# A mixture-of-experts block: one visit loop split in two, with the routed bias products made at the split

## The chip, the core and the metric

The kernel runs on one core of a Trainium2 chip. The core's engines run side by side, each with its own queue: TensorE (PE) multiplies into eight PSUM banks, VectorE (DVE) and ScalarE (ACT) work on vectors, GpSimd (POOL) issues gathers and scatters, SyncE (SP) issues the large transfers. They meet through semaphores. The metric is the device time of one execution in microseconds (us); lower is better. A difference of under 0.3% (4.2 us) can't be told from none here.

## What is computed

One hybrid decoder layer on 512 tokens of 1024 values. Its first part (a gated DeltaNet group and a convolution group) ends before the stretch that matters here. The second part is a mixture of 32 experts, of which each token uses four:

```python
logits = (xt @ w_router + b_router)
top_val, top_idx = lax.top_k(logits, TOP_K)
gates = jax.nn.softmax(top_val, axis=-1)
...
hid = x_blk @ w_gate_up[e] + b_gate_up[e]        # 1024 x 2048 weights per expert
gate, up = hid[:, :D_FF], hid[:, D_FF:]
...
return ((up + 1.0) * glu) @ w_down[e] + b_down[e]  # 1024 x 1024 weights per expert
...
y = jax.ops.segment_sum(weighted, row_tok, num_segments=t + 1)[:t]  # sum of gate * expert output
```

All data are float32. Every expert's 12.6 MB of weights is read once, 402 MB in all. The bias of the down projection, weighted by the gates, doesn't depend on the experts' products: summed over a token's experts it is `gates (512 x 32) @ b_down (32 x 1024)`. These are the **routed bias products**.

## The kernel before

The experts are handled in **visits**. Visit i multiplies expert i's gate/up weights (`gate_up(i)`, line 2138, matmuls in line 2136) and then expert i-1's down weights (`down(i - 1)`, line 2200, matmuls in line 2189). A visit's tokens lie in up to four groups of 32; groups 2 and 3 are skipped where the expert has too few tokens, so visits differ in length on PE. Visit 0 stands alone, visits 1 to m = 30 are one hardware loop on each engine, and the last expert, 31, is handled behind it.

- **SP** issues the weights in a fixed order: for a visit four gate/up pieces c0, c2, c4, c6 of 2 MB into `ring`, then two down pieces of 2 MB (chunk pairs u 0-1 and 2-3) into `dslots`. Each issue waits until PE has used what stood in that slot one expert ago (semaphores `gu_used`, `d_used`), so at most one expert's weights are under way or unused at a time. Behind the loop the order is c0, c2 of expert 31 (these are its first two waits), the down pieces of expert 30, c4, c6, then expert 31's down weights as four pieces of 1 MB. Then come four "planes": 2 MB each of the scattered expert outputs, read back for the final sum (lines 463, 465, 468, and 471 as four tiles).
- **PE** runs `gate_up`, waits for `act_ready`, runs `down`. Bank 6 also takes the small products that turn the routing into row numbers (`idx_mm`, line 2100, between c4 and c6 of a visit), which DVE reads right after (lines 1510 to 1514).
- **DVE** makes row numbers, transposes the gate/up results (line 1575) and the next tokens (1488), and computes the activation; its last step of a visit (line 1615) waits for the down products of the expert before.
- **ACT** makes the sigmoid (line 1007) and scales the down results out of banks 4 and 5 (line 1001, `results`).
- **POOL** gathers tokens and scatters results (lines 621, 626).

The routed bias products need `gates_turn` (four transposes of the gates, line 2111, into bank 7), a copy by ACT (line 1018), and for each of the four token tiles two matmuls into banks 6 and 7 (`routed_bias`, line 2122) and two additions by DVE into `x2` (`add_bias`, lines 1552 and 1553). Since both banks are used again for each tile, PE waits for the additions of the tile before (`acc_ready`). In the kernel before all of it stands behind the loop, among the last expert's gate/up products, while SP's last weights are still arriving.

Of the kernel before, what the change touches and what calls it, by code (L numbers as in the profile page):

```python
# [33 lines left out]
GROUPS = 4  # L34
CAP = GROUP * GROUPS
STAGES = 4


def block_kernel(nc, x, attn_norm_w, w_in, gdn_conv_w, gdn_a_log, gdn_dt_bias, gdn_norm_w, cf_dw_w, cf_dw_b,
# [10 lines left out]
    T = SEQ // P  # L50
# [21 lines left out]
    with ExitStack() as ctx:  # L72
# [98 lines left out]
        def take(*dims):  # L171
# [117 lines left out]
        gt_done, gt_copied, bd_done, acc_ready = (sem(n) for n in ("gt_done", "gt_copied", "bd_done", "acc_ready"))  # L289
        hot_ready, idx_done, idx_ready, gathered, xt_ready = (sem(n) for n in (  # L290
            "hot_ready", "idx_done", "idx_ready", "gathered", "xt_ready"))
# [60 lines left out]
        def tokens_left(engine, i):  # L352

            return engine.value_load(left[0:1, bass.ds(i, 1)], min_val=0, max_val=SEQ)
# [364 lines left out]
        def _(act):  # L719
# [275 lines left out]
            m = visits_less_two(act)  # L995

            def results(stage):

                gates = slot_gate.rearrange("p s g -> p (s g)")
                for g in range(GROUPS):  # L1000
                    ins = A(yb[:, g, :], bank[4 + g // 2][:, (g % 2) * QD:(g % 2 + 1) * QD], ACT.Copy,  # L1001
                            scale=gates[:, bass.ds(stage * GROUPS + g, 1)])
                ins.then_inc(y_ready, 1)
# [5 lines left out]

            act.sem_inc(y_ready, 1)  # L1010
            sigmoid_gate(1)
            with act.Fori(1, m + 1) as i:
                sigmoid_gate(i + 1)
                act.wait_ge(d_used, i * 4 + 4)
                act.wait_ge(landed, i * 16)
                results((i - 1) % STAGES)
            act.wait_ge(gt_done, 1)
            A(GT, bank[7][0:E, :], ACT.Copy).then_inc(gt_copied, 1)
            act.wait_ge(d_used, m * 4 + 8)
            act.wait_ge(landed, m * 16 + 16)  # L1020
            results((E - 2) % STAGES)
# [23 lines left out]
        def _(dve):  # L1045
# [504 lines left out]
            def add_bias(t):  # L1550
                dve.wait_ge(bd_done, t + 1)
                V.tensor_tensor(x2[:, t, 0:HALF], BIAS_PAIR[0][:, :], x2[:, t, 0:HALF], ALU.add)
                V.tensor_tensor(x2[:, t, HALF:D], BIAS_PAIR[1][:, :], x2[:, t, HALF:D], ALU.add
                                ).then_inc(acc_ready, 1)
# [11 lines left out]
            m = visits_less_two(dve)  # L1566
# [19 lines left out]
            def act_part(e, visit, base):  # L1586

                s = own.s
                c = base
                dve.wait_ge(hid_ready, visit * GROUPS + GROUPS)  # L1590

                def biased(out, half):
                    bias = bgu[:, half * KC:(half + 1) * KC, bass.ds(e, 1)]
                    bias = bias.rearrange("p b o -> p (b o)").rearrange("p (b o) -> p b o", o=1)
                    for g in range(GROUPS):
                        V.tensor_tensor(out[:, g, :].rearrange("p (b s) -> p b s", b=KC),  # L1596
                                        hidT[:, g, half, :].rearrange("p (b s) -> p b s", b=KC),
                                        bias.to_broadcast([P, KC, GROUP]), ALU.add).then_inc(s, 1)

                biased(g2, 0)  # L1600
                c = c + GROUPS
                dve.wait_ge(s, c)
                V.tensor_scalar(g2, g2, LIMIT, None, ALU.min).then_inc(g2_ready, 1)  # L1603
                biased(u2, 1)
                c = c + GROUPS
                dve.wait_ge(s, c)
                V.tensor_scalar(u2, u2, LIMIT, -LIMIT, ALU.min, ALU.max).then_inc(s, 1)
                c = c + 1
                dve.wait_ge(sg_ready, visit)
                V.tensor_tensor(g2, g2, sg, ALU.mult).then_inc(s, 1)  # L1610
                c = c + 1
                dve.wait_ge(s, c)
                dve.wait_ge(d_used, visit * 4)
                flat = lambda v: v.rearrange("p g n -> p (g n)")
                V.scalar_tensor_tensor(out=flat(actT), in0=flat(u2), scalar=1.0, in1=flat(g2), op0=ALU.add,  # L1615
                                       op1=ALU.mult).then_inc(act_ready, 1)
# [2 lines left out]
            LOOP_OWN = STEPS_IDX + STEPS_ACT  # L1619
            act_part(0, 1, own.n)  # L1620
            own.n += STEPS_ACT
            with dve.Fori(1, m + 1) as i:
                base = (i - 1) * LOOP_OWN + own.n
                dve.wait_ge(idx_done, i + 3)
                dve.wait_ge(rows_known, i * 2 + 1)
                numbers(base, (i + 2) % STAGES)

                e3 = (i + 3) % E
                hot(e3)
                dve.wait_ge(hot_ready, (i + 4) * (T + 1) - 1)  # L1630
                lower(e3)
                hid_turn(i + 1)
                xt_turn(i + 1)
                act_part(i % E, i + 1, base + STEPS_IDX)

            def last_act():

# [44 lines left out]
                        turn_at[g + 1] = turn(g + 1)  # L1682
                    product(g)

            for t in range(T):
                add_bias(t)
            dve.wait_ge(gu_used, m * KC + 2 * KC)
            dve.wait_ge(d_used, m * 4 + 4)
            last_act()
# [28 lines left out]
        def _(pe):  # L1718
# [389 lines left out]
            def gates_turn():  # L2108
                pe.wait_ge(cnt_read, 1)
                for t in range(T):  # L2110
                    ins = TR(bank[7][0:E, t * P:(t + 1) * P], Gm[:, t, :], ident)
                ins.then_inc(gt_done, 1)
# [83 lines left out]
            def down(i, tokens):  # L2196
                for u in range(4):
                    if u == 1:
                        pe.wait_ge(slot_in[8 + u], 16)
                    elif u % 2 == 0:  # L2200
                        pe.wait_ge(slot_in[8 + u], i * 16 + 16)
                    with pe.If(tokens > 2 * GROUP):
                        down_mm(u, 2)
                        with pe.If(tokens > 3 * GROUP):
                            down_mm(u, 3)
                    down_mm(u, 0)
                    down_mm(u, 1).then_inc(d_used, 1)
# [1 line left out]
            tokens = tokens_left(pe, 0)  # L2209
            pe.wait_ge(xt_ready, 1)  # L2210
            gate_up(0, first=True, known=tokens)
            with pe.Fori(1, m + 1) as i:
                pe.wait_ge(xt_ready, i + 2)
                gate_up(i)
                pe.wait_ge(act_ready, i)
                pe.wait_ge(y_ready, i)
                tokens = tokens_left(pe, i - 1)
                down(i - 1, tokens)
            tokens = tokens_left(pe, m + 1)
            pe.wait_ge(xt_ready, m + 3)  # L2220
            pe.wait_ge(idx_ready, m + 3)
            gates_turn()
            gate_up(m + 1, pairs=(0,), known=tokens)
            routed_bias(0)
            gate_up(m + 1, pairs=(2,), known=tokens)
            routed_bias(1)
            pe.wait_ge(act_ready, m + 1)
            pe.wait_ge(y_ready, m + 1)
            down(m, tokens_left(pe, m))
            routed_bias(2)  # L2230
            gate_up(m + 1, pairs=(4,), known=tokens)
            routed_bias(3)
            gate_up(m + 1, pairs=(6,), known=tokens)

            def last_down(u, g):
                w = view(ring, u * SLOT, 2, D)
# [57 lines left out]
```

## Time and profile before

| | |
|---|---|
| median of three runs | 1394.98 us (1392.49 to 1396.18) |
| span of the profiled execution | 1395.8 us |
| PE busy | 1241.0 us (89%), of it line 2136 566.6, line 2189 284.7 |
| DVE, POOL, ACT busy | 679.5, 320.3, 223.3 us |
| moved by DMA | 455.33 MB, 326 GB/s over the span |
| PE idle until gate/up weights, down weights | 56.2, 21.8 us |
| granted TensorE clock, mean | 0.973 of 2.4 GHz |

The profile is of one execution, and its span runs from the first to the last instruction; the page gives no other time for it. It lies 0.8 us above the median and within the range of the runs. Its times within the span are used as they are, and differences found in them are applied to the median. In the rows, a timeline row has its start and its length in us, then engine, line, operation, tiles and count, and in square brackets how long the engine had been idle and what released it. PE's matmul ends are modelled.

### The profile page before, as it was taken

How to read it: one execution, taken by the hardware profiler on the slowest of the kernel's cores; microseconds unless marked ns; L12 is line 12 of the kernel's file. 1: busy time of each engine (PE TensorE's matmuls, PEld its weight loads, DVE VectorE, ACT ScalarE, POOL GpSimd, SP SyncE). 2: the span in 40 equal slices, each digit the busy share in tenths (PEclk: the TensorE clock that was granted, in tenths of full speed). 3: DMA queues.
4: the chain of work that ended last, by engine and by line, in shares of the span. 5: the costliest groups of instructions: out<-in, count | busy, mean ns of one | idle time of the engine just before them, and what ended most of it. 6: DMA issues, size and time to landing. Idle time of an engine off the chain costs nothing.

```text
span 1395.8 us, 32044 instructions
## 1 busy us (share of the span) xinstructions
PE 1241.0 (89%) x12814; PEld 585.9 (42%) x12815; DVE 679.5 (49%) x1360; ACT 223.3 (16%) x439; POOL 320.3 (23%) x432
## 2 busy tenths in 40 slices
PE   6999999999599999899899999798978887879992
PEld 3444454564235554353534445233432332335331
DVE  2898885444644364335434433345443334353428
ACT  3125543412100011000000100000110000001103
POOL 5001111000322224222223212222233222222221
PEclk9999999999799999999999999999999999999996
DMA  9212000312589999999999999999999999999996
GB/s 307 85 61 91 1 31 1 142 74 86 210 337 400 409 418 424 425 426 426 426 425 425 424 426 425 426 426 425 426 424 425 426 427 425 426 426 426 380 407 245
DMA packets 59374, 455.33 MB, mean 326 GB/s; under 512 B 13308, under 2 KB 23604, under 8 KB 34214
## 3 DMA queue, kind: packets, MB, share of 16 engines
q1 hardware_dynamic: 44262, 432.59, 74.8%
q0 software_dynamic: 11568, 18.92, 3.7%
q10 hardware_dynamic: 3504, 3.26, 0.9%
q8 instruction: 28, 0.46, 0.1%
q14 instruction: 12, 0.10, 0.0%
HBM read 445.02 MB, written 14.81 MB: 329 GB/s over the span
## 4 chain that ended last, share of the span: by engine, by line
PE 58%; DMA 29%; DVE 7%; issue 2%; ACT 2%; ACTq 1%; POOL 0%; SPq 0%; DVEq 0%; POOLq 0%
PE bank L2136 26%; DMA ring<-in_w_gate_up_dram 15%; PE bank L2189 14%; DMA dslots<-in_w_down_dram 14%; PE bank L1797 6%; PE bank L1987 4%; DVE dslots L1122 3%; PE bank L1792 2%; DVE hbuf L1697 1%; PE bank L1865 1%; PE bank L1872 1%; PE bank L2100 1%; PE bank L2122 1%; PE bank L1952 1%; PE bank L1956 1%
## 5 line engine op out<-in xcount | busy, mean ns | idle before, releaser
L2136 PE MATMUL bank<-ring,wq 128*32 128x512 f32 x4992 | 566.6, 601 | 64.9 <-DMA ring<-in_w_gate_up_dram 56.2
L2136 PEld LDWEIGHTS bank<-ring,wq 128*32 128x32 f32 x4992 | 208.8, 111 | 381.1 <-issue 344.3
L2189 PE MATMUL bank<-dslots,intra 128*32 128x256 f32 x5056 | 284.7, 380 | 22.6 <-DMA dslots<-in_w_down_dram 21.8
L2189 PEld LDWEIGHTS bank<-dslots,intra 128*32 128x32 f32 x5056 | 169.1, 110 | 148.3 <-issue 54.6
L1510 DVE TENSOR_REDUCE small<-bank 128x4 f32<-128x8 f32 x33 | 5.5, 166 | 409.8 <-PE bank L2100 409.8
L1007 ACT ACTIVATE zrows<-intra 128x1024 f32<-128x1024 f32 x31 | 32.8, 1059 | 790.0 <-DVE intra L1603 763.8
L1797 PE MATMUL bank<-hbuf,ring 128*128 128x512 f32 x320 | 148.5, 604 | 0.7 <-ACT hbuf L748 0.7
L616 POOL COPY idx_in<-idx 128x4 int32 (+1 forms) x32 | 11.8, 370 | 555.6 <-DVE wq L1488 534.4
L1575 DVE STREAM_TRANSPOSE wq<-bank 128x512 f32<-128x512 f32 x124 | 77.8, 685 | 71.7 <-PE bank L2136 71.7
L621 POOL DMA_INDIRECT wq<-xn_rows,idx_in x82 | 100.5, 1225 | 44.3 <-POOL idx_in L616 28.0
L626 POOL DMA_INDIRECT y_rows<-rows,idx_out x79 | 81.0, 1025 | 52.5 <-POOL idx_out L616 25.2
L1122 DVE SCALAR_TENSOR_TENSOR dslots<-dslots,small 128x512 f32<-128x512 f32 x120 | 89.9, 781 | 0.7 <-DVE small L1091 0.2
L1797 PEld LDWEIGHTS bank<-hbuf,ring 128*128 128x128 f32 x320 | 57.3, 190 | 59.9 <-issue 56.6
L1488 DVE STREAM_TRANSPOSE wq<-wq 128x1024 f32<-128x1024 f32 x31 | 63.3, 2041 | 10.5 <-DMA wq<-xn_rows,idx_in 10.5
L1001 ACT ACTIVATE rows<-bank,small 128x256 f32<-128x256 f32 x124 | 48.7, 476 | 100.1 <-PE bank L2189 94.3
L1987 PE MATMUL bank<-ring,dslots 128*128 128x512 f32 x128 | 60.8, 609 | 0.3 <-DVE dslots L1254 0.3
L1615 DVE SCALAR_TENSOR_TENSOR intra<-zrows,intra 128x1024 f32<-128x1024 f32 x31 | 38.0, 1225 | 35.2 <-PE bank L2189 32.1
L633 POOL DMA_DIRECT2D spare<-in_gdn_dt_bias_dram x93 | 51.9, 565 | 0.1
L1596 DVE TENSOR_TENSOR zrows<-wq,small 128x256 f32<-128x256 f32 x124 | 44.2, 419 | 0.0
L1479 DVE TENSOR_SCALAR rows<-slot_no,small 128x512 bf16<-128x512 bf16 x136 | 39.2, 351 | 9.8 <-DVE place L1514 9.3
L1596 DVE TENSOR_TENSOR intra<-wq,small 128x256 f32<-128x256 f32 x124 | 43.3, 415 | 0.0
L554 POOL TENSOR_TENSOR sqbuf<-qkbuf 128x512 f32<-128x512 f32 x8 | 11.8, 1471 | 122.4 <-DVE qkbuf L1164 122.4
(294 smaller groups left out, 894.4 us busy)
## 6 DMA issues: line engine op xcount, KB each, us to landing
ring<-in_w_gate_up_dram SPq DMA_DIRECT2D x127, 2048.0 KB
dslots<-in_w_down_dram SPq DMA_DIRECT2D x61, 2048.0 KB
ring<-in_w_in_dram SPq DMA_DIRECT2D x12, 1024.0 KB, 13.5
ring<-in_w_out_dram SPq DMA_DIRECT2D x4, 1024.0 KB, 5.6
ring<-in_w_down_dram SPq DMA_DIRECT2D x4, 1024.0 KB
dslots<-y_rows SPq DMA_DIRECT2D x2, 2048.0 KB, 20.1
hbuf<-in_x_dram SPq DMA_DIRECT2D x4, 512.0 KB, 5.4
dslots<-in_w_down_dram SPq DMA_DIRECT2D x2, 1024.0 KB, 4.7
```

The costliest lines, as they stand in the source:

```text
L621: pool.indirect_dma_start(out=xg[:, g, :], out_offset=None, in_=xn_q, in_offset=bass.IndirectOffsetOnAxis(ap=numbers[:, g:g + 1], axis=0), ...
L626: pool.indirect_dma_start(out=y_q, out_offset=bass.IndirectOffsetOnAxis(ap=numbers[:, g:g + 1], axis=0), in_=y[:, g, :], in_offset=None, b ...
L633: pool.dma_start(spare[0:1, k * H:(k + 1) * H], gdn_dt_bias[0:1, :]).then_inc(done, 16)
L1001: ins = A(yb[:, g, :], bank[4 + g // 2][:, (g % 2) * QD:(g % 2 + 1) * QD], ACT.Copy, scale=gates[:, bass.ds(stage * GROUPS + g, 1)])
L1122: own.mark(V.scalar_tensor_tensor(out=cacc[:, j, :], in0=ubuf[:, j, k:k + SEQ], scalar=PT[:, j, k:k + 1], in1=cacc[:, j, :], op0=ALU.mult, ...
L1488: V.transpose(xT.rearrange("p g (c s) -> p g c s", c=KC), xg.rearrange("p g (r c) -> p g c r", c=KC)).then_inc(xt_ready, 1)
L1575: V.transpose(hidT[:, g, :, :].rearrange("p h (c s) -> p h c s", c=KC), bank[g][:, :].rearrange("p (h r c) -> p h c r", h=2, c=KC)).then_i ...
L1596: V.tensor_tensor(out[:, g, :].rearrange("p (b s) -> p b s", b=KC), hidT[:, g, half, :].rearrange("p (b s) -> p b s", b=KC), bias.to_broad ...
L1797: ins = M(bank_of(s)[:, :], unit_ap(u)[:, c, half * P:(half + 1) * P], hT[:, c, :], start=(c == 0), stop=(c == KC - 1))
L1987: ins = M(pair[half][:, :], lhs, w, start=(kc == 0), stop=(kc == KC - 1))
L2136: ins = M(bank[g][GROUP * j:GROUP * (j + 1), :], x[:, g, c * GROUP:(c + 1) * GROUP], w[:, :, j * QD:(j + 1) * QD], start=(c == 0), stop=(c ...
L2189: ins = M(b[GROUP * j:GROUP * (j + 1), col:col + QD], actT[:, g, c * GROUP:(c + 1) * GROUP], w[:, cc, j * QD:(j + 1) * QD], start=(c == 0 ...
```

## The change

The body of the visit loop becomes a function on PE, DVE and ACT, and the loop stands twice: visits 1 to 15 and visits 16 to 30 (SP's and POOL's loops stay whole). Between the two, PE makes the four transposes and the eight matmuls of the routed bias in a row, waiting after each tile for DVE, and waits at the end for the last addition; ACT copies the turned gates there, and DVE makes the additions there. All of this is gone behind the second loop.

```diff
@@ ACT
-            with act.Fori(1, m + 1) as i:
+            def visit(i):
                 sigmoid_gate(i + 1)
                 act.wait_ge(d_used, i * 4 + 4)
                 act.wait_ge(landed, i * 16)
                 results((i - 1) % STAGES)
+
+            with act.Fori(1, MID) as i:
+                visit(i)
             act.wait_ge(gt_done, 1)
             A(GT, bank[7][0:E, :], ACT.Copy).then_inc(gt_copied, 1)
+            with act.Fori(MID, m + 1) as i:
+                visit(i)
@@ DVE
+            with dve.Fori(1, MID) as i:
+                visit(i)
+            for t in range(T):
+                add_bias(t)
+            with dve.Fori(MID, m + 1) as i:
+                visit(i)
...
-            for t in range(T):
-                add_bias(t)
             dve.wait_ge(gu_used, m * KC + 2 * KC)
@@ PE
+            with pe.Fori(1, MID) as i:
+                visit(i)
+            pe.wait_ge(idx_ready, MID + 2)
+            gates_turn()
+            for t in range(T):
+                routed_bias(t)
+            pe.wait_ge(acc_ready, T)
+            with pe.Fori(MID, m + 1) as i:
+                visit(i)
             tokens = tokens_left(pe, m + 1)
             pe.wait_ge(xt_ready, m + 3)
-            pe.wait_ge(idx_ready, m + 3)
-            gates_turn()
-            gate_up(m + 1, pairs=(0,), known=tokens)
-            routed_bias(0)
-            gate_up(m + 1, pairs=(2,), known=tokens)
-            routed_bias(1)
+            gate_up(m + 1, pairs=(0, 2), known=tokens)
             pe.wait_ge(act_ready, m + 1)
             pe.wait_ge(y_ready, m + 1)
             down(m, tokens_left(pe, m))
-            routed_bias(2)
-            gate_up(m + 1, pairs=(4,), known=tokens)
-            routed_bias(3)
-            gate_up(m + 1, pairs=(6,), known=tokens)
+            gate_up(m + 1, pairs=(4, 6), known=tokens)
```

`MID = 16`. On PE, behind the loop of the kernel before, the gates' transposes stand ahead of the last expert's c0, and the first bias products between c0 and c2 (in the names, `kbg` holds the gates, `vbuf` the turned gates, `qkbuf` the down biases; a row ends with the semaphores it waits for):

```order
L2111 MATMUL bank<-consts,kbg 32x128 [waits cnt_read,idx_ready,xt_ready]
L2111 MATMUL bank<-consts,kbg 32x128 x3
...
L2168 REGISTER_ALU
L2136 MATMUL bank<-ring,wq 32x512 [waits hid_ready]
L2136 MATMUL bank<-ring,wq 32x512 x7
L2122 MATMUL bank<-qkbuf,vbuf 128x512 [waits gt_copied,bias_in]
L2122 MATMUL bank<-qkbuf,vbuf 128x512
L2155 COMPARE_AND_BRANCH [waits slot_in2]
L2136 MATMUL bank<-ring,wq 32x512 x8
```

In the changed kernel PE has them between the end of the first loop (line 2231, `Fori`'s branch) and the start of the second:

```order
L2231 COMPARE_AND_BRANCH
L2122 MATMUL bank<-consts,kbg 32x128 [waits cnt_read,idx_ready]
L2122 MATMUL bank<-consts,kbg 32x128 x3
L2133 MATMUL bank<-qkbuf,vbuf 128x512 [waits gt_copied,bias_in]
L2133 MATMUL bank<-qkbuf,vbuf 128x512
L2133 MATMUL bank<-qkbuf,vbuf 128x512 [waits acc_ready]
L2133 MATMUL bank<-qkbuf,vbuf 128x512
...
L2238 UNCONDITIONAL_BRANCH [waits acc_ready]
L2238 ISA
L355 ISA [waits xt_ready]
```

The bias products are no longer interleaved with gate/up products: three of the four tiles start with a wait for `acc_ready` and so does the branch into the second loop, with nothing else in PE's queue to run meanwhile.

On ACT the copy of the turned gates, which stood behind the whole loop, now stands behind the scaling of visit 15 and ahead of visit 16's sigmoid:

```order
L1002 ACTIVATE rows<-bank,small 128x256
L1019 REGISTER_ALU
L1019 COMPARE_AND_BRANCH
L1022 ACTIVATE vbuf<-bank 32x512 [waits gt_done]
L1023 UNCONDITIONAL_BRANCH
L1023 ISA
L1008 ACTIVATE zrows<-intra 128x1024 [waits g2_ready]
```

So PE's first bias product waits for ACT's scaling of expert 14's down results as well.

## Rows read from the trace of the kernel before

**Rows 1.** The page's slices: GB/s moved in 40 equal slices of 34.9 us.

```profile
GB/s 307 85 61 91 1 31 1 142 74 86 210 337 400 409 418 424 425 426 426 426 425 425 424 426 425 426 426 425 426 424 425 426 427 425 426 426 426 380 407 245
```

**Rows 2.** Waits of PE, 876 to 1325 us: total us, times, longest.

```profile
PE bank L2136 <- DMA ring<-in_w_gate_up_dram: 42.1, 32, 2.3
```

**Rows 3.** Timeline of PE from the end of visit 15: start, length, [idle, releaser].

```profile
862.21 10.66 PE L2136 MATMUL bank<-ring,wq 128*32 128x512 f32 x96
...
884.15 3.66 PE L2189 MATMUL bank<-dslots,intra 128*32 128x256 f32 x64 [1.05 <-DMA dslots<-in_w_down_dram]
889.10 3.77 PE L2136 MATMUL bank<-ring,wq 128*32 128x512 f32 x32 [1.29 <-DMA ring<-in_w_gate_up_dram]
...
900.77 5.34 PE L2136 MATMUL bank<-ring,wq 128*32 128x512 f32 x32 [2.05 <-DMA ring<-in_w_gate_up_dram]
```

**Rows 4.** Timeline of SP's queue: c0 of expert 17 and the three behind.

```profile
866.24 11.73 SPq L401 DMA_DIRECT2D ring<-in_w_gate_up_dram  x4
```

**Rows 5.** The page's DMA issues with size and median us to landing.

```profile
dslots<-in_w_down_dram SPq DMA_DIRECT2D x2, 1024.0 KB, 4.7
...
ring<-y_rows SPq DMA_DIRECT2D x1, 2048.0 KB, 17.1
```

**Rows 6.** Timeline of DVE behind the loop.

```profile
1330.78 0.69 DVE L1552 TENSOR_TENSOR hbuf<-bank,hbuf 128x512 f32<-128x512 f32 x1 [4.82 <-PE bank L2122]
1331.39 0.68 DVE L1553 TENSOR_TENSOR hbuf<-bank,hbuf 128x512 f32<-128x512 f32 x1
...
1357.85 0.72 DVE L1652 STREAM_TRANSPOSE wq<-bank 128x512 f32<-128x512 f32 x1 [2.41 <-PE bank L2136]
...
1377.33 4.63 DVE L1697 TENSOR_TENSOR hbuf<-hbuf,ring 128x1024 f32<-128x1024 f32 x4
```

**Rows 7.** Timeline of ACT behind the loop: the copy of the turned gates.

```profile
1326.33 0.57 ACT L1018 ACTIVATE vbuf<-bank 32x512 f32<-32x512 f32 x1
```

**Rows 8.** Timeline of PE behind the loop.

```profile
1314.04 10.54 PE L2189 MATMUL bank<-dslots,intra 128*32 128x256 f32 x192
1324.67 0.60 PE L2111 MATMUL bank<-consts,kbg 128*32 128x128 f32 x4
...
1328.76 1.98 PE L2122 MATMUL bank<-qkbuf,vbuf 32*128 32x512 f32 x4
...
1336.15 10.57 PE L2189 MATMUL bank<-dslots,intra 128*32 128x256 f32 x192
...
1354.04 3.64 PE L2136 MATMUL bank<-ring,wq 128*32 128x512 f32 x32
1361.29 8.80 PE L2240 MATMUL bank<-ring,intra 128*32 128x256 f32 x128 [3.61 <-DVE intra L1675]
```

**Rows 9.** Windows: length, PE, PEld, DVE, ACT, POOL busy, PEclk, DMA share, GB/s.

```profile
901.30:904.70 3.40, 3.40 (x24) 0.84 (x20) 0.00 (x0) 0.00 (x0) 0.00 (x0) 0.50 0.98 419
```

**Rows 10.** The same view, behind the loop.

```profile
1318.00:1320.00 2.00, 2.00 (x44) 1.22 (x40) 2.00 (x5) 0.00 (x0) 0.38 (x1) 1.00 0.48 205
```

**Rows 11.** The chain that ended last: start, us, what; c4 of expert 30.

```profile
1277.98 24.94 DMA ring<-in_w_gate_up_dram
```

**Rows 12.** Timeline of SP's queue: planes 0, 2 and 3.

```profile
1346.78 0.38 SPq L463 DMA_DIRECT2D dslots<-y_rows  x1
...
1358.00 0.36 SPq L468 DMA_DIRECT2D ring<-y_rows  x1
1377.36 1.76 SPq L471 DMA_DIRECT2D ring<-y_rows  x4
```

**Rows 13.** Planes 0 and 1 (tile dslots, behind the loop): us from issue to landing.

```profile
DMA to landing us min/median/max: 17.8/20.1/22.3
```

**Rows 14.** DMA queues with packets in 445 to 1300 us; all of them.

```profile
q1 hardware_dynamic: 23925, 348.51, 96.3%
q0 software_dynamic: 9269, 14.17, 4.5%
```

**Rows 15.** The page's DMA queues, whole span: the larger queue of instructions.

```profile
q8 instruction: 28, 0.46, 0.1%
```

More of the change, by code:

```diff
@@ L36 @@
 STAGES = 4
+MID = 16
 def block_kernel(nc, x, attn_norm_w, w_in, gdn_conv_w, gdn_a_log, gdn_dt_bias, gdn_norm_w, cf_dw_w, cf_dw_b,
@@ L1621, in _, with visit @@
             own.n += STEPS_ACT
-            with dve.Fori(1, m + 1) as i:
+            def visit(i):
                 base = (i - 1) * LOOP_OWN + own.n
@@ L2211, in _, with visit @@
             gate_up(0, first=True, known=tokens)
-            with pe.Fori(1, m + 1) as i:
+            def visit(i):
                 pe.wait_ge(xt_ready, i + 2)
```

## The prediction

> **What bounds the kernel now.** I read the page's slices first. From about 450 us on, the core moves 424 to 427 GB/s in every slice until the last three [rows 1]. The visit loop is bound by the stream of weights, and PE only follows it: after 876 us it waited 32 times for gate/up weights, 42.1 us in all, never over 2.3 us at once [rows 2]. Next I read how far the stream runs ahead of PE. Piece c4 of expert 30 was issued at 1277.98 and landed 24.94 us later [rows 11]. Then I looked at how fast the last engine of the stream goes, since PE waits for the last part of a piece. From that landing (1302.92) to the landing of plane 0 (issued 1346.78, 17.8 us to landing: 1364.6 [rows 12, 13]) SP's order has nine 2 MB pieces behind c4, four of 1 MB, and plane 0: twelve units of 2 MB in 61.7 us, **5.14 us a unit**. In between, mean DMA share fell to 0.48 [rows 10], and yet that pace was kept. So part of the DMA engines had run out of work there, and the slowest had not. That is what I cost by: the slowest engine's queue must not run dry, and idle time of the faster ones is free.
>
> Last I read the end. PE shows no idle from 1314.04 to 1357.7 [rows 8], so PE looks like the bound of the tail. Behind it DVE starts at 1357.85 and works without a break until 1381.96 [rows 6], where the last plane is added and the final norm begins.
>
> **The tail: what goes.** Removed from PE there are four transposes, 0.60 us, and four bias tiles of 1.98 us: 8.5 us [rows 8]. The additions by DVE (0.69 and 0.68 us a tile) and ACT's copy lay beside PE's work and give nothing. But the weights don't come sooner. With 5.14 us a unit from 1302.9, c2 of expert 31 lands at 1328.6, the down pieces of expert 30 at 1333.8 and 1338.9, c4 and c6 of 31 at 1344.1 and 1349.2, the four last down pieces at 1351.8, 1354.3, 1356.9 and 1359.5, and planes 0 and 1 at 1364.6 and 1369.7. Plane 2 landed at 1358.00 + 17.1 = 1375.1 [rows 5, 12].
>
> Walking PE through that: `down(29)` ends at 1324.6 as before; c0 takes 3.6 to 1328.2; c2 is there at 1328.6 and done at 1332.2. The first half of `down(30)` starts when its piece lands, 1333.8, and ends at 1339.1; the second half is there and ends at 1344.3 (before: 1346.7). c4 to 1347.9; c6 waits until 1349.2 and ends at 1352.8, against 1357.7: **4.9 us earlier**, not 8.5. The last expert's down products start 3.4 us after that, as before (1361.29 against 1357.85 [rows 6, 8]), but the first group then waits for the last piece, 1359.5, and ends at 1360.1; three more groups of 2.2 (8.80 / 4) give 1366.7, against 1370.1: 3.4 us earlier. DVE's activation is through at about 1363.3. Then its twelve additions (4.63 us for a plane) wait for the planes: plane 0 from 1364.6, plane 1 from 1369.7, plane 2 from 1375.1 to 1379.7, against 1381.96. So the tail gives **2.2 us**, because the planes stand behind the weights in the same queues, and plane 2 is late next. A second thing may cap that. Plane 3 was issued at 1377.36 [rows 12], 7.3 us after PE's last product, when the last scatter had landed; now that scatter would run while plane 2 still moves, and may take a few us more. If it lands no earlier than before, a gain of about 1 remains. I take 2.0. The bounds are 0.8 and 4.9 us (the latter if the planes came as much earlier as PE). Nothing in the removal can cost time at this place.
>
> **The middle: what is added.** Nobody else has work for PE there. PE's stretch between visits 15 and 16 is a chain. ACT's scaling of the down results and the copy of the gates end at 1326.90 in the tail, 2.3 us after the down products' end at 1324.58 [rows 7, 8], and the same order stands in the middle. Each tile then takes 2.02 us to the start of DVE's additions (1328.76 to 1330.78), 1.29 us for both additions (to 1332.07), and some 0.1 for the semaphore: 3.4 us [rows 6, 8]. With 0.1 ahead of the first tile, four tiles and 2.4 make X = 16.0; the code around it (leaving one loop, entering another) costs 0 to 1.1, and I take 0.3. **X = 16.3 us** of delay for everything PE does from 862.2 on [rows 3].
>
> What hides it is the stream's lead. The second down piece of expert 15 landed at 884.1, where PE began on it after a DMA wait [rows 3]. The next piece in SP's order is c0 of expert 17, issued at 866.24 [rows 4], as soon as PE had used c0 of expert 16, and landed at 889.1 [rows 3]. An issue needs 2.2 us before data flow: 1 MB landed in 4.7 us [rows 5], of which 2.5 are transfer at 424 GB/s. So the slowest engine runs dry if that issue is later than 884.1 - 2.2 = 881.9, that is, if the delay is over **15.6 us**. With X = 16.3 the stream loses 0.7 us. From then on PE's two-group pieces take 3.64 to 3.77 us against 5.17 of the stream, and PE waits for gate/up weights 42 us in all until 1325 [rows 2, 3], so the 16 us are made up within some six visits and the tail meets PE as before.
>
> The term without a row is TensorE's clock in that chain, where PE is busy 2 us and idle 1.4 in turn. The trace shows that short idles can be enough: after idles of 2.2 and 2.05 us between pieces the granted clock was 0.50 from 901.3 to 904.7, which is 1.2 GHz, and the piece there took 5.34 us instead of 3.64 [rows 3, 9]. Such a stretch costs 1.7 us in solid work, some 1.2 where PE works 60 to 70% of the time. Ends: none (0), or the whole chain and the first piece at 1.2 GHz (4 x 1.98 + 1.7 = 9.6). I take one stretch, 1.2 us, nearest to what idles of this length did here. The middle costs 0.7 + 1.2 = **1.9 us**.
>
> The Trainium skill (TensorE: Matmul & The Clock Gate, section on psum-queue depth-cycling) tells of a kernel in which small idles between matmul groups made the clock fall again and again. By that, the whole chain would run at the lower level, which is the clock rival below; this trace has the fall at 901.3 for it, and idles of 1.29 and 1.05 us without a fall against it.
>
> **Sum.** +1.9 - 2.0 = -0.1 us on the median of 1394.98: **1394.9**.
>
> **Rivals.**
> - *The tail pays in full.* If PE and not the stream bounds the tail, 8.5 us go and the middle costs 1.9 at most: 1394.98 - 8.5 + 1.9 = 1388.4. For it speaks PE without idle time [rows 8]; against it the landings at 5.14 us a unit up to plane 0. Chance 0.06.
> - *The clock (slower).* PE at 1.2 GHz through the chain: X = 16.3 + 7.9 = 24.2, the first piece 1.7 more, the stream dry for 24.2 + 1.7 - 15.6 = 10.3, less 2.0 from the tail: 1403.3. It decides from a loss of 6.2 us, that is X of about 21.8; three stretches at the low clock and a slow loop entry would do. Chance 0.13, with what lies between it and the forecast.
> - *Code.* PE's loop body now stands a second time, at another place in memory. If its turn had to load code, each of 15 turns would stop PE. I price a turn at one unit of the stream, 5.1 us, as if the load waited behind one piece; PE's waits give back 42 us of the 77, so 35 would stay: 1430. Against it: in 445 to 1300 us, some 28 turns, only the two data queues have packets [rows 14], though the instruction queue had 28 in all [rows 15]; the body is held, and the second one has the same size. Chance 0.05. The Trainium skill (Runtime: NRT & Kernel Launch, section Instruction fetch mechanics) says that a taken branch to code outside the engine's buffer waits for a DMA, and gives PE a buffer of 2048 instructions; the trace agrees so far as the first loop needs no packet.
> - *No effect of the split:* the chain is fully hidden and the planes are last anyway: 1394.98 - 2.0 = 1393.0. This lies inside the forecast's own range, 1391.5 to 1398, which has a chance of 0.76 together.
>
> **Numbers.** Within 0.3% is 1390.8 to 1399.2. Faster than that: the full tail, 0.06, and 0.01 of the rest. Slower: clock 0.12 of its 0.13, code 0.05, and 0.02 for a piece of the chain that I don't see: 0.19. Same: 0.74. The range reaches from 1391.5, the forecast's low end (tail 3.5, middle 0), to 1401, most of the way to the full clock case; it leaves out the full tail, the code case and the upper part of the clock case.
>
> **What would show it.** In the changed profile, PE should have the eight bias matmuls at about 865 to 878 us with DVE's additions between, and 16 us between the end of `down(14)` and c0 of expert 16. DMA share should dip at about 876 to 885 for a moment, since the faster engines run out of work some us sooner, with the first wait of PE for weights back after some six visits. The page's clock row should show at most a short fall near 870. In the tail PE should now wait for weights (a DMA wait of about 1.5 us ahead of `down(30)` and another ahead of c6), end its gate/up products 4 to 5 us earlier relative to `down(29)`, and DVE should wait ahead of the planes. I am wrong if DMA share is low for over 10 us in the middle and everything behind is late by more than 4 us, if PE idles at each turn of the second loop, or if PE's tail runs without waits for weights and the planes land earlier by as much.

## The result, and the profile after

The change is slower. The median of five runs is 1403.55 us (1402.74 to 1405.84) against 1396.18 us for the kernel before, run beside it; the ratio is **1.0056, 95% interval 1.0046 to 1.0067**, or +7.8 us (the two medians by themselves differ by 7.4). One run of the kernel before, taken beside the first experiments, lasted 3265 us and is left out of the ratios. The prediction said 1394.9 us, no change, with a range up to 1401.0: it was wrong. The profiled executions differ by 8.2 us (spans 1404.0 and 1395.8).

The page of the changed kernel shows where, in its slices of 35.1 us (DMA share in tenths, then GB/s):

```profile
DMA  9212000311589999999999999699999999999996
GB/s 311 79 61 91 1 31 1 155 67 79 223 348 398 413 421 425 423 428 426 425 424 423 426 426 424 272 424 424 428 425 423 426 425 427 426 425 426 420 409 266
```

Against [rows 1] one slice stands out, 272 GB/s instead of 424: the stream of weights stood still for part of it, between 878 and 913 us, where the loops meet. Its slices behind that are full again. The prediction's last part names this as a sign of being wrong, and it is nearly the whole result.

PE's timeline around the split (start, length, idle before and releaser):

```profile
847.48 14.02 PE L2200 MATMUL bank<-dslots,intra 128*32 128x256 f32 x256 [1.44 <-DMA dslots<-in_w_down_dram]
861.43 0.61 PE L2122 MATMUL bank<-consts,kbg 128*32 128x128 f32 x4
863.96 2.36 PE L2133 MATMUL bank<-qkbuf,vbuf 32*128 32x512 f32 x4 [1.92 <-ACT vbuf L1022]
867.71 3.78 PE L2133 MATMUL bank<-qkbuf,vbuf 32*128 32x512 f32 x4 [1.38 <-DVE hbuf L1559]
872.86 3.77 PE L2133 MATMUL bank<-qkbuf,vbuf 32*128 32x512 f32 x4 [1.38 <-DVE hbuf L1559]
878.02 3.78 PE L2133 MATMUL bank<-qkbuf,vbuf 32*128 32x512 f32 x4 [1.38 <-DVE hbuf L1559]
884.30 12.95 PE L2147 MATMUL bank<-ring,wq 128*32 128x512 f32 x96 [2.50 <-issue]
897.18 0.55 PE L2111 MATMUL bank<-rows 128*128 x16
```

The chain is the one that was forecast, in its order and with its waits (1.38 us for DVE each time), but three of the four tiles take 3.78 us where [rows 8] had 1.98. Windows of the same stretch (length; PE, PEld, DVE, ACT, POOL busy; PEclk, DMA share, GB/s) say why, and what it did to the stream:

```profile
866.00:884.00 18.00, 11.65 (x13) 3.48 (x12) 5.15 (x8) 0.00 (x0) 2.97 (x3) 0.50 0.73 308
884.00:890.00 6.00, 5.70 (x32) 1.47 (x36) 0.00 (x0) 0.00 (x0) 0.00 (x0) 0.56 0.01 3
...
876.00:878.00 2.00, 0.64 (x1) 0.00 (x0) 1.29 (x2) 0.00 (x0) 0.00 (x0) 0.50 0.82 340
878.00:880.00 2.00, 1.98 (x3) 0.94 (x4) 0.00 (x0) 0.00 (x0) 0.00 (x0) 0.50 0.48 205
880.00:882.00 2.00, 1.79 (x3) 0.22 (x1) 0.17 (x1) 0.00 (x0) 0.00 (x0) 0.50 0.21 90
```

The first tile began at a granted clock of 1.00 and the clock fell within it (2.36 us); from 866 us to the end of the chain, and in the first products behind it, the clock is 0.50 (1.2 GHz). From 877 us the DMA share falls step by step, as one engine after another runs out of work, and from 884 to 890 it is 0.01. SP's queue has the matching gap:

```profile
854.83 7.19 SPq L409 DMA_DIRECT2D dslots<-in_w_down_dram  x2
890.64 7.14 SPq L402 DMA_DIRECT2D ring<-in_w_gate_up_dram  x3
```

c0 of expert 17 is issued at 890.64, against 866.24 in [rows 4]. In this execution PE was through with `down(14)` 0.8 us earlier than before (the next work starts at 861.43 against 862.21), so the issue is 24.4 + 0.8 = 25.2 us late, against a lead of 15.6.

Behind it PE caught up sooner than forecast. Its first wait for gate/up weights comes at 960.85 us, 77 us behind the chain: some two and a half visits, where the prediction said six.

The tail, PE and then DVE's additions of the planes:

```profile
1333.12 7.15 PE L2147 MATMUL bank<-ring,wq 128*32 128x512 f32 x64
1341.85 5.39 PE L2200 MATMUL bank<-dslots,intra 128*32 128x256 f32 x96 [1.57 <-DMA dslots<-in_w_down_dram]
...
1354.41 7.07 PE L2147 MATMUL bank<-ring,wq 128*32 128x512 f32 x64 [1.58 <-issue]
1365.10 9.78 PE L2253 MATMUL bank<-ring,intra 128*32 128x256 f32 x128 [3.61 <-DVE intra L1688]
```

```profile
1373.61 4.63 DVE L1708 TENSOR_TENSOR hbuf<-hbuf,dslots 128x1024 f32<-128x1024 f32 x4 [1.47 <-DMA dslots<-y_rows]
1378.65 4.63 DVE L1708 TENSOR_TENSOR hbuf<-hbuf,dslots 128x1024 f32<-128x1024 f32 x4 [0.41 <-DMA dslots<-y_rows]
1385.55 4.63 DVE L1708 TENSOR_TENSOR hbuf<-hbuf,ring 128x1024 f32<-128x1024 f32 x4 [2.27 <-DMA ring<-y_rows]
```

Everything here is 8.7 us later than before, by the end of `down(29)` (1333.3 against 1324.6). Less that, PE ends its gate/up products at 1352.8, to the tenth what was forecast, and DVE now waits for each plane, where in [rows 6] it worked without a break. It is through the third plane at 1390.18, against 1381.96: 8.2 later, so the tail gave 0.5 us.

### The profile page after: what moved, and what is told of

It reads as the page before. It is cut to its first block, busy times and chain, and to the rows that moved or that the text cites. A ratio compares the mean times of both kernels' runs of the same rounds, so it can differ in the third digit from the quotient of the medians.

```text
span 1404.0 us, 32047 instructions
## 1 busy us (share of the span) xinstructions
PE 1251.1 (89%) x12814; PEld 557.2 (40%) x12815; DVE 680.2 (48%) x1360; ACT 222.6 (16%) x439; POOL 321.1 (23%) x432
## 4 chain that ended last, share of the span: by engine, by line
PE 55%; DMA 33%; DVE 6%; issue 2%; ACT 2%; ACTq 1%; POOL 0%; SPq 0%; POOLq 0%; DVEq 0%
PE bank L2147 24%; DMA ring<-in_w_gate_up_dram 20%; PE bank L2200 12%; DMA dslots<-in_w_down_dram 11%; PE bank L1808 5%; PE bank L1998 4%; DVE dslots L1128 3%; PE bank L1803 2%; DMA ring<-y_rows 1%; PE bank L2133 1%; PE bank L1876 1%; PE bank L1883 1%; PE bank L1963 1%; PE bank L2111 1%; PE bank L1967 1%
## 5 line engine op out<-in xcount | busy, mean ns | idle before, releaser
L2147 PEld LDWEIGHTS bank<-ring,wq 128*32 128x32 f32 x4992 | 180.5, 111 | 403.1 <-issue 393.6
L2200 PE MATMUL bank<-dslots,intra 128*32 128x256 f32 x5056 | 281.7, 379 | 23.4 <-DMA dslots<-in_w_down_dram 21.5
## 6 DMA issues: line engine op xcount, KB each, us to landing
dslots<-y_rows SPq DMA_DIRECT2D x2, 2048.0 KB, 22.9
```

The costliest lines, as they stand in the source:

```text
L2147: ins = M(bank[g][GROUP * j:GROUP * (j + 1), :], x[:, g, c * GROUP:(c + 1) * GROUP], w[:, :, j * QD:(j + 1) * QD], start=(c == 0), stop=(c ...
L2200: ins = M(b[GROUP * j:GROUP * (j + 1), col:col + QD], actT[:, g, c * GROUP:(c + 1) * GROUP], w[:, cc, j * QD:(j + 1) * QD], start=(c == 0 ...
```

## Experiments

All compare with runs of the kernel before on the same chip. **Theory**: PE's stop between the loops is free as long as it is shorter than the lead of the stream, 15.6 us at this place; beyond it each us costs one. The stop was too long since TensorE ran at 1.2 GHz. A ratio nearer to 1 than the 0.3% of the opening is read with its interval, and only as a small shift. **Rivals**: the second copy of the loop costs by itself (code); the chain with DVE, or the clock, costs directly; any stop costs its length.

### The loop twice, nothing else

```diff
-            with pe.Fori(1, m + 1) as i:      # and on DVE and ACT
-                visit(i)
+            with pe.Fori(1, 16) as i:
+                visit(i)
+            with pe.Fori(16, m + 1) as i:
+                visit(i)
```

> The loop stands twice on PE, DVE and ACT as in the changed kernel, but the routed bias products stay behind the loop, as in the kernel before. Theory (the stream of weights ran dry because PE was stopped for over 15.6 us between visits 15 and 16): entering a second loop stops PE for 1 to 3 us, far less than the lead, so the time is that of the kernel before, 1396 us within 1.5. Rival (the second copy of the loop costs by itself, through loading its code at the start or at each turn): 2 to 8 us slower than before, with most of the change's 7.8 us in it.

Ratio 1.0003 (0.9994 to 1.0012). The second copy is free. In the changed kernel's own trace the queue of instructions does have packets within the loops, unlike [rows 14] (445 to 1300 us):

```profile
q8 instruction: 5, 0.08, 0.0%
```

Four of the five lie between 880 and 930 us, around the first pass of the second loop, one between 445 and 600, and none at the turns behind 930. The run of the split alone has five as well, four of them between 862 and 900, and no cost. So code is loaded once; the rival "code" of the prediction falls.

### The bias products left out

```diff
-            gates_turn()
-            gate_up(m + 1, pairs=(0,), known=tokens)
-            routed_bias(0)
-            gate_up(m + 1, pairs=(2,), known=tokens)
-            routed_bias(1)
+            gate_up(m + 1, pairs=(0, 2), known=tokens)
...
-            routed_bias(2)
-            gate_up(m + 1, pairs=(4,), known=tokens)
-            routed_bias(3)
-            gate_up(m + 1, pairs=(6,), known=tokens)
+            gate_up(m + 1, pairs=(4, 6), known=tokens)
```

> One loop, and the routed bias products, their copy and their additions are left out altogether; the rest is as in the kernel before. It leaves the bias of the down projection out of the sum. It shows what the removal from the tail is worth alone. Theory (the planes stand behind the weights in the same queues, so DVE waits for plane 2): 0.5 to 2 us faster, 1394.2 to 1395.7, with PE's gate/up products 4.9 us earlier. Rival (PE bounds the tail): 8.5 us faster, 1387.7.

Ratio 0.9995 (0.9986 to 1.0004): 0.7 us less at best guess, at most 2.0, and not to be told from none. PE bounding the tail (8.5 us) is ruled out. PE is early and waits for weights, DVE waits for planes:

```profile
1329.61 5.39 PE L2184 MATMUL bank<-dslots,intra 128*32 128x256 f32 x96 [1.64 <-DMA dslots<-in_w_down_dram]
...
1345.33 3.64 PE L2131 MATMUL bank<-ring,wq 128*32 128x512 f32 x32 [1.21 <-DMA ring<-in_w_gate_up_dram]
```

```profile
1360.84 4.63 DVE L1692 TENSOR_TENSOR hbuf<-hbuf,dslots 128x1024 f32<-128x1024 f32 x4 [1.21 <-DMA dslots<-y_rows]
1365.88 4.63 DVE L1692 TENSOR_TENSOR hbuf<-hbuf,dslots 128x1024 f32<-128x1024 f32 x4 [0.41 <-DMA dslots<-y_rows]
1372.72 4.63 DVE L1692 TENSOR_TENSOR hbuf<-hbuf,ring 128x1024 f32<-128x1024 f32 x4 [2.21 <-DMA ring<-y_rows]
```

The third starts 6.84 us after the second, though a plane needs 5.1 us of the stream.

### The same, with the final norm's weights loaded earlier

```diff
+            act.dma_start(finw, final_norm_w...).then_inc(late_in, 16)
             act.wait_ge(d_used, m * 4 + 8)
...
-            act.dma_start(finw, final_norm_w...).then_inc(late_in, 16)   # behind the last results
```

> As the run without the bias products (they and their additions are left out), with ACT's load of the final norm's weights (512 KB) issued right behind the loop instead of behind the last expert's results. In that run plane 2 landed 6.8 us after plane 1, against 5.5 in the kernel before, and took back 1.4 us of the tail's gain. Theory (that load and the last scatter now run between planes 1 and 2): with the load out of the way plane 2 lands about 5.5 us after plane 1, but everything from the planes on is about 1.2 us later, so the time is that of the run without the bias products within 1 us. Rival (the last scatter alone does it): plane 2 still 6.8 us after plane 1, and 1 us slower.

Ratio 0.9994 (0.9985 to 1.0003), the same as without that edit. DVE's additions:

```profile
1369.35 4.63 DVE L1692 TENSOR_TENSOR hbuf<-hbuf,dslots 128x1024 f32<-128x1024 f32 x4 [0.46 <-DMA dslots<-y_rows]
1374.60 4.63 DVE L1692 TENSOR_TENSOR hbuf<-hbuf,ring 128x1024 f32<-128x1024 f32 x4 [0.62 <-DMA ring<-y_rows]
```

Plane 2 now follows plane 1 by 5.25 us. So it was the 512 KB load, not the last scatter, that slid in ahead of plane 2 once ACT came to it earlier. In the time it makes no difference that can be measured: issued earlier, the load holds up the weights instead (PE waits 2.92 us ahead of `down(30)`, against 1.64 in the run before).

### Clock: matmuls in the waits

```diff
+                    for _ in range(2):      # ahead of tile 0, while ACT copies
+                        M(bank[0][:, :], consts[:, 0:P], consts[:, 0:512], start=True, stop=True)
...
                 ins.then_inc(bd_done, 1)
+                M(bank[0][:, :], consts[:, 0:P], consts[:, 0:512], start=True, stop=True)
...
+            pe.wait_ge(hid_ready, MID * GROUPS + GROUPS)      # ahead of the gates' transposes
```

The last line, which the two runs with four pairs of banks have as well, keeps the new products out of banks that DVE still reads. It added no stop: in all three traces the transposes start as `down(14)` ends.

> The changed kernel with extra matmuls of constants (128x128 by 128x512) into the idle bank 0 on PE: two ahead of the first bias tile and one behind each tile, in PE's waits for ACT and DVE; their results aren't used. Theory (the chain took 22.9 us instead of 16.3 because TensorE ran at 1.2 GHz in it): the granted clock stays at 1.0, a bias tile takes 1.98 us, PE is stopped for 17 to 18 us, the stream is dry for 2, and the time is 1397 to 1398.5. Rival (the clock fell along with something else that cost the time, such as code loading or a wait for DVE): the extra work changes nothing or adds to it, 1403 or more.

Ratio 1.0002 (0.9993 to 1.0011): **adding** work to PE took all of the change's loss away. The first, a middle and the last piece of the stop:

```profile
861.31 1.95 PE L2135 MATMUL bank<-qkbuf,vbuf 32*128 32x512 f32 x4 [0.17 <-ACT vbuf L1022]
863.19 1.12 PE L2138 MATMUL bank<-consts 128*128 128x512 f32 x2
864.65 1.98 PE L2135 MATMUL bank<-qkbuf,vbuf 32*128 32x512 f32 x4 [0.33 <-DVE hbuf L1559]
...
875.86 10.51 PE L2150 MATMUL bank<-ring,wq 128*32 128x512 f32 x96 [1.45 <-issue]
```

A tile takes 1.98 us again, PE is stopped for 17.1 us (858.8 to 875.9) instead of 22.9, and c0 of expert 17 is issued 16.9 us late, 1.3 over the lead.

### Clock: no waits between the tiles

```diff
-        BIAS_PAIR = (bank[6], bank[7])
+        BIAS_PAIRS = [(bank[0], bank[1]), (bank[2], bank[3]), (bank[4], bank[5]), (bank[6], bank[7])]
...
-                if t >= 1:
-                    pe.wait_ge(acc_ready, t)
```

> The changed kernel, with a pair of banks for each bias tile (0-1, 2-3, 4-5, 6-7) instead of banks 6 and 7 for all four: PE no longer waits for DVE's additions between tiles, only at the end. Theory: PE is stopped for 2.4 + 7.9 + 1.4 + 1.2 = 12.9 us, under the lead of 15.6, the stream doesn't run dry, and the time is before's less what the tail gives, 1395.7 (1394 to 1397). Rival (any stop of this kind costs its length once, since PE has no slack): about 1396.2 + 12.9 - 0.5 = 1408; or, if bank order is not it, no change from 1403.6.

Ratio 1.0019 (1.0009 to 1.0028): better than the change, worse than before, and not as expected. PE's row of all eight products, and the window in it:

```profile
863.35 13.72 PE L2131 MATMUL bank<-qkbuf,vbuf 32*128 32x512 f32 x16 [1.89 <-ACT vbuf L1022]
```

```profile
864.00:877.00 13.00, 13.00 (x16) 4.65 (x14) 3.87 (x6) 0.00 (x0) 4.05 (x4) 0.50 0.99 418
```

PE is busy for 13.00 of 13.00 us, and the granted clock is 0.50 all the same. So the idle times between the tiles are not what held the clock down. PE was stopped for 18.7 us, not the 12.9 of the forecast. These products contract over 32 rows, a quarter of the array's; that was the next suspect.

### Clock: the same products over 128 rows

```diff
+            V.memset(vbuf[:, :], 0.0).then_inc(gt_cleared, 1)   # rows 32 to 127 of the turned gates are zero
...
-  M(BIAS_PAIR[half][:, :], GT[:, t * P:(t + 1) * P], bdn[:, half * HALF:(half + 1) * HALF], ...
+  M(BIAS_PAIR[half][:, :], GT_all[:, t * P:(t + 1) * P], bdn_all[:, half * HALF:(half + 1) * HALF], ...
```

> The changed kernel, with the bias products contracted over 128 rows instead of 32: DVE clears the whole of the turned gates' tile first, so rows 32 to 127 add zeros. PE's waits between the tiles stay. In the run with four pairs of banks the clock was at 1.2 GHz although PE had no idle time between the bias products. If what lowers it is that these matmuls fill only 32 of 128 rows, the clock stays at 2.4 GHz here even with the waits, PE is stopped for 17.5 us, the stream is dry for about 2, and the time is 1 to 2 us above before. If the waits lower it by themselves, a tile takes 3.8 us again and the time is that of the change, 0.5% above before.

Ratio 1.0015 (1.0004 to 1.0026), 2.1 us, of the change's 7.8. The time is near the forecast, but not for its reason alone, since the clock did not stay up:

```profile
863.08 2.81 PE L2137 MATMUL bank<-qkbuf,vbuf 128*128 128x512 f32 x4 [2.20 <-ACT vbuf L1025]
867.27 3.75 PE L2137 MATMUL bank<-qkbuf,vbuf 128*128 128x512 f32 x4 [1.38 <-DVE hbuf L1562]
872.41 1.98 PE L2137 MATMUL bank<-qkbuf,vbuf 128*128 128x512 f32 x4 [1.38 <-DVE hbuf L1562]
875.77 1.98 PE L2137 MATMUL bank<-qkbuf,vbuf 128*128 128x512 f32 x4 [1.38 <-DVE hbuf L1562]
```

The clock still fell, behind the 2.20 us wait for ACT, but with the same 1.38 us waits going on it **came back** for the last two tiles. In the change and with four pairs, over 32 rows, it came back only in the gate/up products behind the chain. How long the clock is low varies here: the profiled execution (1400.87 us, mean clock 0.965) is one of the two slowest of twelve, and the fastest (1394.71 us) had a mean of 0.976. So the stop of 20.0 us in this trace is longer than in most of the runs.

> Both together: 128 rows, and a pair of banks for each tile, so no wait between tiles. Theory of the rows: clock at 2.4 GHz, eight products in 7.9 us, PE stopped for 12.9 us, under the lead of 15.6: the stream isn't dry, and the time is before's or up to 1 us less. Otherwise (the clock falls with any run of these products): as the run with four pairs, 0.2% above before.

Both edits together: ratio 0.9999 (0.9988 to 1.0009). All eight products take 8.80 us instead of 13.72 (the clock was 0.50 from 864 to 867 us, so not the 7.9 of the forecast), and PE is stopped for 14.2 us (859.6 to 873.8), less than the lead:

```profile
862.45 8.80 PE L2135 MATMUL bank<-qkbuf,vbuf 128*128 128x512 f32 x16 [2.20 <-ACT vbuf L1025]
873.79 12.20 PE L2149 MATMUL bank<-ring,wq 128*32 128x512 f32 x96 [2.54 <-issue]
```

### The lead: a stop of plain matmuls

```diff
             with pe.Fori(1, MID) as i:
                 visit(i)
+            for _ in range(12):      # or 24
+                M(bank[7][:, :], consts[:, 0:P], consts[:, 0:512], start=True, stop=True)
```

> The loop stands twice and the bias products stay in the tail, as in the run of the split alone; between the loops PE makes 12 matmuls of constants (128x128 by 128x512) into bank 7, about 11.3 us of solid work at 2.4 GHz with no wait on any engine. PE is stopped for 12.5 us. Theory of the lead: less than 15.6, so no cost, the time is before's within 1 us. Rival (each us of PE's stop costs one): 12 us slower.

Ratio 1.0002 (0.9992 to 1.0012): 10.5 us of extra PE work cost nothing.

> The same with 24 such matmuls, 22.6 us, PE stopped for 23.8 us. Theory of the lead: 23.8 - 15.6 = 8 us slower than before, 0.6%, though no bias product, no wait for ACT or DVE and no low clock is in it, and DMA share near 0 for some 8 us. Rival (the cost of the change came from the low clock or from the chain with DVE as such): no more than 2 us slower.

Ratio 1.0051 (1.0033 to 1.0069), +7.1 us with 4.6 to 9.6 as its interval (the medians by themselves differ by 5.4), at full clock and with no wait for another engine. The matmuls took 20.87 us, 0.87 each rather than the 0.94 that was assumed:

```profile
860.55 20.87 PE L2234 MATMUL bank<-consts 128*128 128x512 f32 x48
881.35 10.51 PE L2147 MATMUL bank<-ring,wq 128*32 128x512 f32 x96
```

The issue of c0 is 20.7 us late, 5.1 over the lead. So the first 10.5 us are free and more than half of the next 10 are not. The low clock matters only through the length of the stop.

### The lead: the same chain at other places

```diff
-MID = 16
+MID = 17      # or 4
```

> The changed kernel with the split one visit later: visits 1 to 16, then the bias products, then 17 to 30. In the trace of before, PE had been waiting for weights in visit 16, so the stream is further ahead: the next piece after it (c0 of expert 18) was issued 19.6 us before the slowest engine would have run dry, not 15.6. Theory of the lead: the same chain at 1.2 GHz delays that issue by some 24 us, the stream is dry for 4.3 instead of 9.4, and the time is 3 to 5 us above before (0.2 to 0.35%). Rival (the cost is that of the chain itself, wherever it stands): 7.8 us as in the change.

> The changed kernel with the split early: visits 1 to 3, then the bias products. There the stream had just begun to run ahead of PE: c0 of expert 5 was issued 4.5 us before the slowest engine would have run dry. Theory of the lead: dry for 25 - 4.5 = 20 us, time 1415 to 1418 (1.4% above before), though nothing else differs from the change. Rival (same cost wherever it stands, or all made up over the 27 visits behind it): 1404 or less.

Split one visit later: ratio 1.0015 (1.0004 to 1.0025), +2.1 us. Split early, behind visit 3: ratio 1.0148 (1.0132 to 1.0163), **+20.7 us**, 1415.89 us (19.6 by the medians). The same chain costs 2, 8 or 21 us, depending on the place. The next issue was late by 22.9, 25.2 and 24.9 us (in the later split the first tile still ran at 2.4 GHz, 1.95 us); less leads of 19.6, 15.6 and 4.5 that is 3.3, 9.6 and 20.4. Read again from the last completion of the piece ahead in the kernel before (509.8 us), the lead of the early split is 3.8 rather than 4.5. The stream in 40 equal slices of 480 to 560 us of the early split:

```profile
GB/s 426 442 410 459 385 426 426 287 354 418 410 434 389 127 0 0 0 0 0 0 0 8 0 139 393 426 459 410 426 434 426 418 434 440 391 424 408 428 426 441
```

Nine slices of 2 us are empty or nearly so. For the later split I expected 3 to 5 us and measured 0.6 to 3.5: the order is right, and the size at the low end. What was forecast for the early one, 1415 to 1418, came.

All stops at the split behind visit 15. "Issued late" is by how much the issue of c0 of expert 17 came later than in the kernel before, counted from the end of `down(14)`; the bytes are what the core moved from 850 to 940 us; the last column is the time of the one profiled execution less the median of the kernel before on that chip:

| kernel | PE stopped, us | issued late, us | MB moved | ratio to before | profiled execution, us |
|---|---|---|---|---|---|
| before | 0 | 0 | 38.28 | 1 | |
| loop twice | 0 | 0.0 | 38.18 | 1.0003 | +0.9 |
| 12 matmuls | 10.5 | 10.4 | 38.04 | 1.0002 | -1.2 |
| 128 rows, four pairs | 14.2 | 15.7 | 37.12 | 0.9999 | -1.4 |
| matmuls in the waits | 17.1 | 16.9 | 36.15 | 1.0002 | -2.5 |
| four pairs | 18.7 | 20.8 | 34.78 | 1.0019 | +3.6 |
| 128 rows | 20.0 | 21.6 | 34.23 | 1.0015 | +4.4 |
| 24 matmuls | 20.8 | 20.7 | 34.68 | 1.0051 | +4.9 |
| the change | 22.9 | 25.2 | 32.72 | 1.0056 | +9.7 |

Up to an issue that is late by about the lead nothing is lost, and beyond it the profiled executions lose roughly the rest. The three rows near 21 us lie 1.3 us apart by their profiled executions and 5 us apart by their ratios. For "128 rows" the trace is of a slow execution, as said above; that "24 matmuls" costs more than "four pairs" is explained by the 0.5 us of the tail only in part, and the rest stays open. 1.2 MB missing costs nothing, and neither do 2.1: those are the faster DMA engines, idle while the slowest still works. In the change 5.56 MB are missing, 13.1 us of all engines at 425 GB/s, of which 7.8 us reach the end.

## Why the prediction was wrong

- **What bounds the kernel; 5.14 us a unit; the slowest engine.** Right (5.17 us in one place of the prediction is a slip for 5.14, and nothing hangs on it). The plain stops and the two other places bear out, within 2 us, that the cost of a stop is its length less the lead, and the forecast of the early split was made from the lead in the trace of before.
- **The length of the chain.** Right up to the clock: 2.5 us to the first tile, 1.29 for the additions, waits of 1.38 us. The entry into the second loop took 1.2 us from DVE's last addition to the first gate/up product (883.1 to 884.3), where I took 0.3 out of 0 to 1.1. Without the clock the delay would have been 17.1 us instead of 16.3.
- **The clock term failed, and with it the forecast.** The prediction took the short idles of the chain to cost one stretch at 1.2 GHz, 1.2 us, between ends of 0 and 9.6. Measured: the four tiles took 13.7 us instead of 7.9, +5.8, and the first piece behind them 6.3 us up to its issue instead of 4.0, +2.3: **8.1 us**, near the far end. I chose by the row of nearest idle time [rows 3, 9], which was the wrong likeness: the loop's rows are of 128-row matmuls, and the bias products fill 32. With four pairs of banks the clock was low for 13 us without any idle time in them; with 128 rows it came back in spite of the idles.
- **The lead of 15.6 us** held within 1 us. 25.2 us of delay less 15.6 is 9.6, and the profiled span grew by 8.2 with 0.5 gained in the tail.
- **The tail.** PE's part was right (4.9 us earlier, with the DMA waits at the forecast places, except that the stop ahead of c4 and c6 was one of PE's own queue, 1.58 us). The gain read from the profiles was 0.5 us instead of 2.0, under my lower bound of 0.8: I had let the last scatter run into plane 2, but not the 512 KB of the final norm, which moved ahead of it and made plane 2 1.7 us later than I had it. The run with that load moved shows it. The two errors of the sum, 6.9 us in the clock and 1.5 in the tail, had the same sign.
- **The rivals.** What happened is the clock rival: it was priced at 1403.3 us, and 1403.55 was measured. That the two agree to 0.3 us is luck: it stood for +8.3 us on a median of 1394.98, with 2.0 from the tail, and the measured +7.8 stands on 1396.18, with 0.5. It had 0.13, and the range, up to 1401, stopped short of it. The full tail and the code rival are ruled out by runs.

Of the Trainium skill's two rules, that of the page TensorE: Matmul & The Clock Gate (psum-queue depth-cycling) pointed the right way, and its reason isn't the whole one here: small idles between groups were not needed to hold the clock down (four pairs), and over 128 rows they did not hold it down. That of Runtime: NRT & Kernel Launch (Instruction fetch mechanics) agrees with the trace: PE's loop body, an estimated 1,060 matmuls and weight loads where all four groups run (256 and 256 records and 16 of `idx_mm`, each with its weight load), is within the 2048 instructions that it gives for PE, and neither loop loads code at its turns.

Open: whether the wait of 1.9 to 2.2 us for ACT starts each fall (it stands ahead of it in every such run, though with the split one visit later the whole first tile still ran at 1.00 and the clock fell behind it; two matmuls in it went with no fall, but they came together with the others); what it is in the 32 rows that keeps the clock low; and what the four pairs with 128 rows are worth against before, since 0.9999 doesn't tell them apart. None of these versions beats the kernel before by a margin that can be measured.

## What to carry to other kernels

- A kernel bound by a prefetched stream takes extra work on its compute engine for free, up to the lead of the stream at that place. Read the lead from the trace as (when the slowest engine would run dry) less (when the next issue is made) less the start-up of a transfer, and put the work where it is largest; past it each us costs about one.
- Work taken out of the tail is worth what the next thing in line leaves of it. Here 8.5 us of PE were worth 0.5 to 0.7 in the profiles, which the runs can't tell from none, because the last loads stand behind the weights in the same queues.
- Price a run of small matmuls at both clock levels when it is put by itself. Between solid products it ran at 2.4 GHz, alone at 1.2.

## What the runs showed of the hardware

- **Rows and the clock.** Matmuls that contract over 32 rows ran at a granted clock of 0.50 for 13 us with PE busy without a gap (four pairs, 864 to 877 us); the same number of matmuls over 128 rows took 8.80 us instead of 13.72. Between gate/up products the 32-row ones ran at full speed (1.98 us a tile [rows 8]). Filling rows with zeros made them faster, and so did extra matmuls in the waits.
- **DMA engines drift apart and are drawn together by a stop.** The sixteen completions of one transfer lie 7.7 us apart in the kernel before at 876 to 884 us, and 15.4 us apart at 1307 to 1323; the mean share fell to 0.48 at 1318 us [rows 10], and the slice there had 380 GB/s [rows 1]. In the changed kernel all engines ran dry at 884 us, the completions at 897 us lie 0.4 us apart, and the late slice has 420. In every run with a stop of 14 us or more near 880 us that slice has 416 to 422, in those without one 380 to 391, and with the early stop at 500 us 391 again. It bought no time that the runs show.
- **Entering a second loop** stopped PE for some 1.2 us where its branch stood behind a wait for DVE, and not at all where PE had matmuls queued ahead of it (24 matmuls: the last ends at 881.42, the first gate/up product starts at 881.35). The first pass stopped PE once for 1.8 us (`issue`, 907.45 us), and once or twice for 0.9 to 3.2 us in the other runs with a stop near 880 us. With the stream ahead, it is free (loop twice, 1.0003).
